# An expert weight ring of eight groups instead of six, with loops over four experts

## The chip, the cores and the metric

The program runs on one core of one Trainium2 chip. The metric is the device time of one execution in microseconds, from the runs of the whole program; the profile is of one such execution. PE is the TensorE (matrix) engine, DVE the VectorE, ACT the ScalarE, POOL the GpSimd engine, and SP the SyncE, which issues most of the DMA transfers. SBUF is the on-chip memory of 128 partitions, PSUM the accumulators of PE (8 banks of 512 fp32 values a partition).

## What is computed

Two blocks on x, 256 tokens of 1024 features, all in fp32. The first block has two attentions, a gated merge, then 32 routed experts and a small gate (PLE); the second block is two layers of convolution and pooling with a modulation made from c. The experts carry most of the weights: each has 1024 x 2048 for gate and up and 1024 x 1024 for down, 12 MB, 402 MB in all.

```python
def hybrid_layer(...):
    ...
    merged = sigmoid(gate_a) * (y_a @ w_branch_a) + sigmoid(gate_b) * (y_b @ w_branch_b)
    x = x + merged @ w_out
    x = x + routed_experts(rmsnorm(x, g_ffn), w_router, b_router, w_gate_up, b_gate_up, w_down, b_down)
    hp = rmsnorm(x, g_ple)
    x = x + sigmoid(hp @ w_ple_gate) * (p_i @ w_ple_proj)

# an expert, on the tokens that chose it (top 4 of 32)
gu = xb @ w_gate_up[e] + b_gate_up[e]
g, u = minimum(gu[:, :1024], 7.0), clip(gu[:, 1024:], -7.0, 7.0)
y = ((u + 1.0) * g * sigmoid(1.702 * g)) @ w_down[e] + b_down[e]

# second block, per layer l
mod = silu(c) @ w_ada[l] + b_ada[l]          # shift, scale, gate
h = rms_norm(x, g_pre[l]) * (1 + scale) + shift
```

## The kernel before

Each engine has its own hand-written program; they meet only through semaphores. SP issues the weight loads in one fixed order, in three phases, through one SBUF tile, ring, of 12 slots of 1 MB (P x 2048 fp32).

- Phase 1 (to about 270 us): the projections, both attentions, the merge, w_out, the router. 48 chunks of 1 MB go through the 12 slots (chunks1, the semaphore chunk_used1 counts those that PE is done with). Among them are 24 chunks of w_ada_2, whose products run between the others on PE (ada_parts) into PSUM bank 7. ACT copies these sums out (ada_out), SP moves them with 16 small DMAs within SBUF (ada_moved, lines 414 to 418), PE adds and transposes them (mod_sums) and DVE makes the columns of the modulation (mod_columns). For layer 0 that is done between the attentions, for layer 1 the moves are issued ahead of the experts and mod_sums and mod_columns run between PLE and the second block (PSUM use "ada1" of phase 3).
- Experts: 12 MB of an expert are six groups of 2 MB (GROUPS): q = 0 to 3 for gate/up, 4 and 5 for down. Group q always goes to slots 2q and 2q+1 of ring, with a semaphore ring2[q]. SP's function expert(e, used) waits for each group until PE has counted chunk_used2 up to the use of the same slots by the expert before, then issues the load. The first expert's groups wait for the phase-1 chunks in the same slots (phase1_left). Behind them SP issues ada_moved(1), then loops over the other 31 experts.
- PE's loop, like those of DVE and ACT, takes two experts a pass (PAIRS): for each, two bias products, the gate/up product over 8 slots of K (side_by_side, line 1551, 64 matmul instructions), the gather of the next pair's tokens (gather), transposes, the down product (32 instructions). Tokens that an expert gets are selected with a one-hot matrix (pick) and its result is scattered back onto X by another product. A loop over more rounds is for experts with over 64 tokens (extra).
- Ahead of the loop: DVE chooses the experts (choose, shares), counts positions, makes pick; PE gathers the first pair's tokens into PSUM pair 1; DVE copies them to xg (gathered, line 1038); PE waits for ada_out, bias_ready, routed, then enters the loop and waits for xg_ready.
- Phase 3: PLE and the two layers, 37 chunks of 1 MB through slots 0 to 7 (chunks3). The first eight wait for the last expert's groups in the same slots.

Besides ring there is the arena, 72 KB a partition, whose regions are reused from phase to phase; view(kb, n) is n fp32 values from kb on. In phase 1 gate A lies at 0 to 8, gate B at 24 to 32, q and k of the second attention from 36 to 48, merged at 48 to 56, scratch SQ from 56, SW from 62, probabilities from 66. In the experts xg, glu, sig, upc, hid, hidT lie from 0 to 14, scat and pickw from 18, esel, bias, then yslot at 40 to 44 and tok_high from 48. raw_bias, the expert biases as loaded, lies at 62. POOL loads raw_bias after y_done (both attentions ready), ACT casts it to bias (line 624), DVE makes its low part (line 1004), then clears yslot and scat, then adds w_out's product to X (x_sum, line 932).

Of the kernel before, what the change touches and what calls it, by code (L numbers as in the profile page):

```python
# [7 lines left out]
S, D = 256, 1024  # L8
HALVES = S // P
# [19 lines left out]
GROUPS = SLOTS // 2  # L29
# [59 lines left out]
def build(nc, t, out):  # L89
# [8 lines left out]
    with ctx:  # L98
# [58 lines left out]
        ada_rows = [view(24, 512), view(36, 512)]  # L157
        ada_mods = [view(26, 512, "p (r n) -> p r n", r=4), view(38, 512, "p (r n) -> p r n", r=4)]
# [21 lines left out]
        lg, mask, ex, em, pm = [SQ[:, 64 * i:64 * i + 64].rearrange("p (a b) -> p a b", a=HALVES) for i in range(5)]  # L180
        top_v = SQ[:, 320:336].rearrange("p (a b) -> p a b", a=HALVES)
        top_f = SQ[:, 336:352].rearrange("p (a b) -> p a b", a=HALVES)
# [25 lines left out]
        pin = view(57, HALVES * 256, "p (a b) -> p a b", a=HALVES)  # L208
        pT = view(59, 2 * S, "p (a b) -> p a b", a=2)
# [32 lines left out]
        ring2 = [sem(f"ring2_{i}") for i in range(GROUPS)]  # L242
# [28 lines left out]
        def used1(name):  # L271
# [9 lines left out]
                             ("o1", 2, used1("o1")), ("fT0", 0, N), ("fT1", 2, N)])  # L281
        ADA_BANK = 7
        U3, _, _ = ordinals([("pT", 2, N), ("pp0", 0, 1), ("pp1", 2, 1), ("hT0", 1, N), ("hT1", 3, N),
                             ("g0", 1, 3), ("g1", 3, 5), ("ada1", 0, N)])
# [109 lines left out]

        def slot1(n, a, b):
            return ring[:, n % SLOTS1, 0:a * b].rearrange("p (a b) -> p a b", a=a)
# [11 lines left out]
        def _(sp):  # L408
# [19 lines left out]
            def expert(e, used):  # L428
                for q in range(GROUPS):
                    used(q)  # L430
                    two = ring[:, 2 * q:2 * q + 2, :]
                    if q < 4:
                        src = gu_v[ds(e, 1), q].rearrange("e p k n -> (e p) k n")
                        sp.dma_start(two, src).then_inc(ring2[q], 16)
                    else:
                        src = dn_v[ds(e, 1), q - 4].rearrange("e p j n -> (e p) j n")
                        sp.dma_start(two.rearrange("p a (b n) -> p (a b) n", b=2), src).then_inc(ring2[q], 16)
# [5 lines left out]
            expert(0, phase1_left)  # L443
            ada_moved(1)
            with sp.Fori(0, E - 1) as before_e:
                expert(before_e + 1, lambda q: sp.wait_ge(s["chunk_used2"], before_e * GROUPS + (q + 1)))
            sp.wait_ge(s["routed"], 1)
            extra = sp.value_load(nextra[0:1, 0:1], min_val=0, max_val=ROUNDS - 1)
            with sp.If(extra > 0):
                with sp.Fori(0, extra) as r:  # L450
                    with sp.Fori(0, E) as e:
                        expert(e, lambda q: sp.wait_ge(s["chunk_used2"],
                                                       r * (E * GROUPS) + e * GROUPS + ((E - 1) * GROUPS + q + 1)))
# [13 lines left out]
        def _(pool):  # L467
# [40 lines left out]
            pool.wait_ge(s["y_done"], 2)  # L508
# [11 lines left out]
            pool.dma_start(pin, t["p"][0, 0].rearrange("(h p) n -> p h n", p=P)).then_inc(s["p_in"], 16)  # L520
            pool.dma_start(invw, t["inv_windows"]).then_inc(s["inv_in"], 16)
            for z, n in ((U, PAD), (Z, 2)):
                G.memset(z[:, :, 0:n], 0.0).then_inc(s["pads_set"], 1)
            power(0, 2)
            filled3(pool, "ada1")
            for z in (WA, WB):
# [1237 lines left out]
```

## Time and profile before

| | us |
|---|---|
| median of 3 runs | 1474.71 |
| lowest and highest | 1472.77, 1475.29 |
| the profiled execution | 1472.31 |
| its span, first to last instruction | 1470.2 |
| PE busy | 1358.9 (92%) |
| DVE, ACT, POOL busy | 424.4, 274.2, 29.3 |
| chain that ended last | PE 58%, DMA 28%, issue 8%, DVE 3% |

Mean granted clock of PE over the span: 0.977 of full speed. A time in the rows is in microseconds from the span's start, if not marked ns. PEld is PE's weight load, SPq the DMA issues of SP. "[1.51 <-DVE ...]" behind an instruction says that its engine sat idle for 1.51 us before it, and which instruction ended that. Of a busy PE the ends are modelled.

### The profile page before, as it was taken

Reading aid. Unit: us, or ns where it says so; the run is one execution under the profiler, and the core shown is the slowest. Engines: PE = TensorE matmul, PEld = TensorE weight load, DVE = VectorE, ACT = ScalarE, POOL = GpSimd, SP = SyncE. Lnnn points to the kernel's source line nnn. Section 1 sums busy time; section 2 is a strip of 40 time slices with the busy share of each in tenths; the row PEclk is TensorE's granted clock in tenths of the full one; section 3 lists DMA queues with packets and bytes.
Section 4 is the critical chain, followed back from the end, with each engine's and each line's share of the span. In section 5 each row is a group of like instructions: output and inputs, shape, how many; then the busy total and the mean of one; then the engine's idle time right before and its main releaser. Section 6 shows DMA issues by size and latency. Waiting matters only on the chain.

```text
span 1470.2 us, 16175 instructions
## 1 busy us (share of the span) xinstructions
PE 1358.9 (92%) x6558; PEld 676.5 (46%) x6558; DVE 424.4 (29%) x656; ACT 274.2 (19%) x387; POOL 29.3 (2%) x46
## 2 busy tenths in 40 slices
PE   4999999899999999999899999998999989898897
PEld 2446544443333333333333333333333336896896
DVE  0416223421122112112111121121111216675773
ACT  2032222211101101101010011010100114532531
POOL 1100010000000000000000000000000000000000
PEclk9999999899999999999999999999999999899999
DMA  8894266699999999999999999999999996355330
GB/s 313 310 344 150 86 209 241 270 407 428 428 428 429 428 429 428 429 429 428 428 428 428 429 428 428 428 428 429 429 428 430 428 412 224 105 181 199 111 119 29
DMA packets 76663, 498.64 MB, mean 339 GB/s; under 512 B 6919, under 2 KB 8282, under 8 KB 52058
## 3 DMA queue, kind: packets, MB, share of 16 engines
q1 hardware_dynamic: 73360, 494.43, 82.2%
q0 software_dynamic: 704, 2.10, 0.4%
q10 hardware_dynamic: 2570, 1.70, 0.4%
q8 instruction: 22, 0.36, 0.1%
q14 instruction: 7, 0.06, 0.0%
HBM read 497.06 MB, written 1.05 MB: 339 GB/s over the span
## 4 chain that ended last, share of the span: by engine, by line
PE 58%; DMA 28%; issue 8%; DVE 3%; ACT 1%; ACTq 0%; POOL 0%; DVEq 0%; SPq 0%; POOLq 0%
PE ps L1551 28%; DMA ring<-in_w_gate_up_dram 28%; PE ps L1323 7%; PE ps L1650 3%; PE ps L1652 3%; PE ps L1651 3%; PE ps L1545 2%; PE ps L1483 2%; PE ps L1467 2%; PE ps L1333 1%; PE ps L1302 1%; PE ps L1532 1%; PE ps L1614 1%; PE ps L1555 1%; ACT arena L651 1%
## 5 line engine op out<-in xcount | busy, mean ns | idle before, releaser
L1551 PE MATMUL ps<-ring,arena 128*64 128x512 f32 x3072 | 697.6, 605 | 38.8 <-DMA ring<-in_w_gate_up_dram 25.6
L1551 PEld LDWEIGHTS ps<-ring,arena 128*64 128x64 f32 x3072 | 213.1, 139 | 487.9 <-issue 400.3
L1082 DVE TENSOR_SCALAR arena<-ps 128x512 f32<-128x512 f32 x32 | 22.1, 692 | 350.2 <-PE ps L1551 350.2
L644 ACT ACTIVATE arena<-arena 128x512 f32<-128x512 f32 x32 | 20.2, 630 | 505.3 <-DVE arena L1082 505.3
L1323 PE MATMUL ps<-ring,HT 128*128 128x512 f32 (+1 forms) x256 | 111.7, 589 | 0.0
L1652 PE MATMUL ps<-arena_highs,w_low 128*128 128x256 f32 x384 | 108.4, 282 | 0.0
L1043 DVE TENSOR_SCALAR esel<-const 128x128 fp32r<-128x128 f32 x49 | 12.6, 285 | 283.3 <-ACT arena L655 145.9
L655 ACT COPY arena<-ps 64x512 f32<-64x512 f32 x64 | 37.2, 581 | 242.1 <-PE ps L1551 241.7
L1061 DVE TENSOR_TENSOR X<-X,ps 128x1024 f32<-128x1024 f32 x34 | 41.4, 1217 | 124.1 <-PE ps L1545 124.1
L1650 PE MATMUL ps<-arena_highs,ring_highs 128*128 128x256 f32 x256 | 72.7, 284 | 1.8 <-DVE HT_r L1120 1.8
L1323 PEld LDWEIGHTS ps<-ring,HT 128*128 128x128 f32 x256 | 48.2, 191 | 54.5 <-issue 54.1
L1652 PEld LDWEIGHTS ps<-arena_highs,w_low 128*128 128x128 f32 x384 | 73.1, 190 | 0.0
L1651 PE MATMUL ps<-HT_r,ring_highs 128*128 128x256 f32 x256 | 72.3, 282 | 0.0
L1545 PE MATMUL ps<-arena 128*128 128x512 f32 x136 | 67.5, 618 | 2.6 <-DVE X L1061 1.3
L1532 PE MATMUL ps<-pick,tok_high 128*128 128x128 f32 x272 | 65.4, 288 | 1.7 <-issue 1.7
L1532 PE MATMUL ps<-pick,tok_low 128*128 128x128 f32 x272 | 64.1, 283 | 0.0
L1532 PEld LDWEIGHTS ps<-pick,tok_high 128*128 128x128 f32 x272 | 53.5, 200 | 14.7 <-issue 14.7
L1103 DVE TENSOR_TENSOR w_low<-ring,ring_highs 128x2048 fp32r<-128x2048 f32 x26 | 58.3, 2286 | 1.0 <-POOL st L498 0.8
L1532 PEld LDWEIGHTS ps<-pick,tok_low 128*128 128x128 f32 x272 | 53.6, 200 | 0.0
L664 ACT CAST ring_highs<-ring 128x2048 fp32r<-128x2048 f32 x26 | 48.2, 1907 | 22.2 <-PE ps L1652 22.2
L1650 PEld LDWEIGHTS ps<-arena_highs,ring_highs 128*128 128x128 f32 x256 | 49.1, 192 | 2.0 <-issue 2.0
L1651 PEld LDWEIGHTS ps<-HT_r,ring_highs 128*128 128x128 f32 x256 | 48.8, 191 | 0.0
(233 smaller groups left out, 1222.7 us busy)
## 6 DMA issues: line engine op xcount, KB each, us to landing
ring<-in_w_gate_up_dram SPq DMA_DIRECT2D x128, 2048.0 KB, 24.2
ring<-in_w_down_dram SPq DMA_DIRECT2D x64, 2048.0 KB, 21.4
ring<-in_w_in_dram SPq DMA_DIRECT2D x38, 1024.0 KB, 7.0
ring<-in_w_ada_dram SPq DMA_DIRECT2D x24, 1024.0 KB, 9.2
ring<-in_w_out_dram SPq DMA_DIRECT2D x12, 1024.0 KB, 6.1
ring<-in_w_ple_gate_dram SPq DMA_DIRECT2D x4, 1024.0 KB, 23.4
ring<-in_w_branch_a_dram SPq DMA_DIRECT2D x2, 1024.0 KB, 9.7
ring<-in_w_branch_b_dram SPq DMA_DIRECT2D x2, 1024.0 KB, 9.8
```

The lines of the kernel that those rows point to most:

```text
L655: last = A.copy(yslot[g][at:at + CAP, :], ps[at:at + CAP, 5, :])
L664: A.copy(high_of(m), slot3(n)).then_inc(s["w_highs"], 1)
L1061: V.tensor_tensor(X[:, h, :], X[:, h, :], flat(3), ALU.add).then_inc(s["sc_used"], 1)
L1103: V.tensor_tensor(slot3(m + 1, w_low), slot3(m + 1), high_of(m).bitcast(fp32), ALU.subtract).then_inc(s["w_lows"], 1)
L1323: last = T.matmul(ps[:, 2 * p + h, 0:n], HT[:, 4 * kh + k, h * P:h * P + P], slot1(c, 4, n)[:, k, :], start=kh + k == 0, stop=4 * kh + k = ...
L1467: last = T.matmul(ps[:, 2 * p + h, :], HT[:, 4 * br + k, h * P:h * P + P], slot1(c, 4, 512)[:, k, :], start=k == 0, stop=k == 3)
L1532: return T.matmul(ps[:, 2 + j, k % 4 * P:k % 4 * P + P], part[:, h, k, :], pick[:, h].rearrange("p e n -> p (e n)"), start=first, stop=h = ...
L1545: last = T.matmul(ps[:, 6 + g, :], scat[:, h, g, :], yslot[g], start=True, stop=True)
L1551: last = T.matmul(ps[at:at + CAP, bank, :], lhsT, w(g), start=False, stop=stop)
L1650: T.matmul(out, lhs[0], rhs[0], start=first, stop=False, skip_group_check=True)
L1651: T.matmul(out, lhs[0], rhs[1], start=False, stop=False, skip_group_check=True)
L1652: return T.matmul(out, lhs[1], rhs[0], start=False, stop=last, skip_group_check=True)
```

## The change

- The groups go round through eight places of 2 MB (BINS) instead of six: load number s of an expert quartet goes to place s mod 8. Places 0 to 5 are the ring, places 6 and 7 (more_bins) are regions of the arena, 32 to 48 and 56 to 72. ring2 has eight semaphores, and PE waits for 16 times the number of loads of that place.
- SP issues the first loads of places 6 and 7 (groups 0 and 1 of expert 1) behind a wait for y_done, ahead of those of places 0 to 5; ada_moved(1) stands behind the sixth load as before. Its loops go over four experts (QUADS, PER_QUAD = 24 groups).
- PE's loop goes over four experts, two pairs one after the other; DVE's and ACT's loops stay at two.
- To free the arena: ada_rows[1] and ada_mods[1] move to 20 and 16, the router's scratch to 24.5, tmp of the merge to 16, yslot to 4 and the experts' other scratch to 8, raw_bias to 0, pin and pT into tabs. As raw_bias now lies over gate A, POOL loads it after merged_done.
- mod_sums and mod_columns of layer 1 leave phase 3 and stand ahead of the expert loop: on PE behind the first gather (in place of the wait for ada_out), on DVE behind gathered(). They use PSUM pair 2 ("mod1").
- POOL clears the pads and loads inv_windows behind w_highs, that is behind the experts.
- The first eight chunks of phase 3 wait for the last uses of places 0 to 3.

```diff
-GROUPS = SLOTS // 2
+GROUPS = 6
+BINS = 8
+QUADS = E // 4
+PER_QUAD = 4 * GROUPS
...
+        scratch = arena[:, 24 * 256 + 128:26 * 256]
...
-        glu, sig, upc, hid, hidT = [view(4 + 2 * i, 512) for i in range(5)]
-        yslot = [view(40 + 2 * i, 512) for i in range(2)]
+        yslot = [view(4 + 2 * i, 512) for i in range(2)]
+        glu, sig, upc, hid, hidT = [view(8 + 2 * i, 512) for i in range(5)]
...
-        raw_bias = view(62, 3 * 512)
+        raw_bias = view(0, 3 * 512)
+        more_bins = [view(32, 2 * SLOT, "p (a b) -> p a b", a=2), view(56, 2 * SLOT, "p (a b) -> p a b", a=2)]
...
+        def bin2(s):
+            b = s % BINS
+            return ring[:, 2 * b:2 * b + 2, :] if b < SLOTS // 2 else more_bins[b - SLOTS // 2]
...
-            def expert(e, used):
-                for q in range(GROUPS):
-                    used(q)
-                    two = ring[:, 2 * q:2 * q + 2, :]
...
+            def load(e, s):
+                q, two = s % GROUPS, bin2(s)
...
+            def quad(e, used):
+                for s in range(PER_QUAD):
+                    used(s)
+                    load(e + s // GROUPS, s)
...
-            expert(0, phase1_left)
-            ada_moved(1)
-            with sp.Fori(0, E - 1) as before_e:
-                expert(before_e + 1, lambda q: sp.wait_ge(s["chunk_used2"], before_e * GROUPS + (q + 1)))
+            sp.wait_ge(s["y_done"], 2)
+            for k in range(GROUPS, BINS):
+                load(1, k)
+            for k in range(PER_QUAD):
+                if k < GROUPS:
+                    phase1_left(k)
+                elif k >= BINS:
+                    sp.wait_ge(s["chunk_used2"], k - BINS + 1)
+                if k < GROUPS or k >= BINS:
+                    load(k // GROUPS, k)
+                if k == GROUPS:
+                    ada_moved(1)
+            with sp.Fori(0, QUADS - 1) as i:
+                quad(i * 4 + 4, lambda k: sp.wait_ge(s["chunk_used2"], i * PER_QUAD + (PER_QUAD + k - BINS + 1)))
...
-                    sp.wait_ge(s["chunk_used2"], extra * (E * GROUPS) + ((E - 1) * GROUPS + n // 2 + 1))
+                    sp.wait_ge(s["chunk_used2"], extra * (E * GROUPS) + (E * GROUPS - BINS + n // 2 + 1))
...
-            pool.wait_ge(s["y_done"], 2)
+            pool.wait_ge(s["merged_done"], 2)
...
+            pool.wait_ge(s["w_highs"], 1)
+            for z, n in ((U, PAD), (Z, 2), (WA, PAD), (WB, PAD)):
+                G.memset(z[:, :, 0:n], 0.0).then_inc(s["pads_set"], 1)
             pool.dma_start(invw, t["inv_windows"]).then_inc(s["inv_in"], 16)
...
             gathered()
+            mod_columns(1, filled(dve, "mod1"), moved1, U1["mod1"][2] + 1)
...
-            mod_columns(1, filled3(dve, "ada1"), moved3, 1)
...
-            pe.wait_ge(s["ada_out"], 8)
+            mod_sums(1, free(pe, "mod1"), full1)
...
-            with pe.Fori(0, extra * PAIRS + PAIRS) as i:
+            def pair_of_experts(i, s0, loaded):
...
-                            pe.wait_ge(ring2[k // 2], n * 16 + 16)
+                            two = loaded(s0 + e * GROUPS + k // 2)
...
+            with pe.Fori(0, extra * QUADS + QUADS) as i:
+                def loaded(k):
+                    pe.wait_ge(ring2[k % BINS], i * (16 * PER_QUAD // BINS) + 16 * (k // BINS + 1))
+                    return bin2(k)
+
+                pair_of_experts(i * 2, 0, loaded)
+                pair_of_experts(i * 2 + 1, 2 * GROUPS, loaded)
...
-            mod_sums(1, U3["ada1"][0], full3)
```

## Rows read from the trace of the kernel before

**Rows 1.** The page: share of the DMA engines in 40 slices, in tenths.
```profile
DMA  8894266699999999999999999999999996355330
```

**Rows 2.** Windows, the long stretch: busy us of each engine, granted clock, DMA share, GB/s.
```profile
320.00:1180.00 860.00, 809.04 (x3714) 309.48 (x3712) 158.43 (x255) 99.18 (x150) 0.00 (x0) 0.98 1.01 429
```

**Rows 3.** Chain that ended last: start us, us, what; the experts.
```profile
329.97 7.96 PE ps L1551 x32
...
497.51 7.09 PE ps L1551 x32
...
521.39 24.79 DMA ring<-in_w_gate_up_dram
...
931.87 25.49 DMA ring<-in_w_gate_up_dram
...
961.23 25.50 DMA ring<-in_w_gate_up_dram
...
1200.31 7.11 PE ps L1551 x32
```

**Rows 4.** Timeline of SP, its DMA issues: start us, us from first to last, line, operation.
```profile
224.05 0.37 SPq L426 DMA_DIRECT2D ring<-in_w_ada_dram  x1
...
269.87 11.64 SPq L418 DMA_DIRECT2D arena<-arena  x16
286.16 12.68 SPq L434 DMA_DIRECT2D ring<-in_w_gate_up_dram  x4
307.48 3.77 SPq L437 DMA_DIRECT2D ring<-in_w_down_dram  x2
```

**Rows 5.** Windows ahead of the loop and in it, columns as in rows 2.
```profile
240.00:252.00 12.00, 12.00 (x35) 5.77 (x34) 1.88 (x4) 1.66 (x4) 0.57 (x1) 1.00 0.10 22
...
282.00:283.00 1.00, 1.00 (x4) 0.24 (x2) 0.00 (x0) 0.00 (x0) 0.00 (x0) 0.50 0.02 3
283.00:284.00 1.00, 1.00 (x4) 0.24 (x2) 0.00 (x0) 0.00 (x0) 0.00 (x0) 0.50 0.00 0
...
284.00:288.00 4.00, 4.00 (x22) 1.32 (x20) 0.00 (x0) 0.00 (x0) 0.00 (x0) 1.00 0.30 66
```

**Rows 6.** Timeline of PE, its first instructions of the expert loop.
```profile
279.56 1.19 PE L1555 MATMUL ps<-bias,esel 128*128 128x512 f32 x2 [1.51 <-DVE arena L1038]
```

**Rows 7.** Timeline of PE, the modulation's sums of layer 0.
```profile
147.41 1.07 PE L1345 MATMUL ps<-const,arena 24*128 24x24 f32 x8
```

**Rows 8.** The biases and their neighbours: timelines of DVE, ACT, PE; DMA landings.
```profile
225.38 1.22 DVE L922 TENSOR_TENSOR arena<-arena 128x1024 f32<-128x1024 f32 x1
...
230.44 1.49 ACT L624 CAST bias<-arena 128x1536 fp32r<-128x1536 f32 x1
...
232.03 3.53 DVE L1004 TENSOR_TENSOR bias<-arena,bias 32x1536 fp32r<-32x1536 f32 x2 [5.42 <-ACT bias L624]
...
236.82 0.48 DVE L1009 MEMSET arena<- 128x512 f32 x1
243.75 1.29 DVE L932 TENSOR_TENSOR X<-X,ps 128x512 f32<-128x512 f32 x2 [6.44 <-PE ps L1483]
...
250.41 1.04 PE L1494 MATMUL ps<-const,X 128*128 128x128 f32 x8
...
L515 POOL DMA_DIRECT2D arena<-in_b_down_dram x4: 511/511/525, 192.7 to 195.8; - x4
...
arena<-in_p_dram POOLq DMA_DIRECT2D x1, 256.0 KB, 5.8
wr<-in_w_router_dram ACTq DMA_DIRECT2D x1, 128.0 KB, 14.4
```

**Rows 9.** Timeline of PE between PLE and the first layer.
```profile
1253.89 3.36 PE L1302 MATMUL ps<-const,HN 128*128 128x128 f32 x16 [6.53 <-DVE HN L1187]
```

**Rows 10.** The chain at the first back edge; the page's queue of instructions.
```profile
337.94 0.66 PE ps L1555 x2
...
q8 instruction: 22, 0.36, 0.1%
```

More of the change, by code:

```diff
@@ L156, in build @@
         hn_flat = HN[:].rearrange("p a b -> p (a b)")
-        ada_rows = [view(24, 512), view(36, 512)]
-        ada_mods = [view(26, 512, "p (r n) -> p r n", r=4), view(38, 512, "p (r n) -> p r n", r=4)]
+        ada_rows = [view(24, 512), view(20, 512)]
+        ada_mods = [view(26, 512, "p (r n) -> p r n", r=4), view(16, 512, "p (r n) -> p r n", r=4)]
         gate = [view(0, HALVES * D, "p (a b) -> p a b", a=HALVES), view(24, HALVES * D, "p (a b) -> p a b", a=HALVES)]
@@ L241, in build @@
         ring1 = [sem(f"ring1_{i}") for i in range(SLOTS1)]
-        ring2 = [sem(f"ring2_{i}") for i in range(GROUPS)]
+        ring2 = [sem(f"ring2_{i}") for i in range(BINS)]
         ring3 = [sem(f"ring3_{i}") for i in range(SLOTS3)]
@@ L426, in _ @@
                 sp.dma_start(slot1(n, a, b), src).then_inc(ring1[n % SLOTS1], 16)
-            def expert(e, used):
-                for q in range(GROUPS):
-                    used(q)
-                    two = ring[:, 2 * q:2 * q + 2, :]
[L432 to L437, printed above, removed]
+            def load(e, s):
+                q, two = s % GROUPS, bin2(s)
+                if q < 4:
+                    src = gu_v[ds(e, 1), q].rearrange("e p k n -> (e p) k n")
+                    sp.dma_start(two, src).then_inc(ring2[s % BINS], 16)
+                else:
+                    src = dn_v[ds(e, 1), q - 4].rearrange("e p j n -> (e p) j n")
+                    sp.dma_start(two.rearrange("p a (b n) -> p (a b) n", b=2), src).then_inc(ring2[s % BINS], 16)
+            def quad(e, used):
+                for s in range(PER_QUAD):
+                    used(s)
+                    load(e + s // GROUPS, s)
             def phase1_left(q):
@@ L450, in _ @@
                 with sp.Fori(0, extra) as r:
-                    with sp.Fori(0, E) as e:
-                        expert(e, lambda q: sp.wait_ge(s["chunk_used2"],
-                                                       r * (E * GROUPS) + e * GROUPS + ((E - 1) * GROUPS + q + 1)))
+                    with sp.Fori(0, QUADS) as i:
+                        quad(i * 4, lambda k: sp.wait_ge(s["chunk_used2"], r * (E * GROUPS) + i * PER_QUAD
+                                                         + (E * GROUPS + k - BINS + 1)))
             for n, (src, a, b) in enumerate(chunks3):
                 if n < SLOTS3:
-                    sp.wait_ge(s["chunk_used2"], extra * (E * GROUPS) + ((E - 1) * GROUPS + n // 2 + 1))
+                    sp.wait_ge(s["chunk_used2"], extra * (E * GROUPS) + (E * GROUPS - BINS + n // 2 + 1))
                 else:
@@ L1005, in _ @@
                                 ).then_inc(s["bias_ready"], 1)
+            dve.wait_ge(s["bias_ready"], 2)
             run(V.memset(posm[:, :, PCOLS:PCOLS + 2], -1.0))
@@ L1583, in _ @@
                         if k % 2 == 0:
-                            pe.wait_ge(ring2[k // 2], n * 16 + 16)
+                            two = loaded(s0 + e * GROUPS + k // 2)
                         x = xg[:, k, e * CAP:e * CAP + CAP]
-                        side_by_side(0, x, lambda g: ring[:, k, g * 512:g * 512 + 512], 0, k == KC - 1)
-                        last = side_by_side(1, x, lambda g: ring[:, k, F + g * 512:F + g * 512 + 512], 0, k == KC - 1)
+                        side_by_side(0, x, lambda g: two[:, k % 2, g * 512:g * 512 + 512], 0, k == KC - 1)
+                        last = side_by_side(1, x, lambda g: two[:, k % 2, F + g * 512:F + g * 512 + 512], 0, k == KC - 1)
                         if k % 2:
@@ L1619, in _ @@
                     for f in range(2):
-                        pe.wait_ge(ring2[4 + f], n * 16 + 16)
-                        w = ring[:, 8 + 2 * f:10 + 2 * f, :].rearrange("p a (b n) -> p (a b) n", b=2)
+                        w = loaded(s0 + e * GROUPS + 4 + f).rearrange("p a (b n) -> p (a b) n", b=2)
                         for j in range(4):
```

21 lines of the change are left out of this document (8 added, 13 removed).

## The prediction

> **What bounds the kernel now.** I read the page's 40 slices first. The DMA line stands at 9 (90% or more) from the ninth slice to the thirty-third and lower before and after [rows 1]: there is one long stretch in which the weights of the experts arrive without a break, and room ahead of it. The window from 320 to 1180 us puts a number on it: 429 GB/s at a DMA share of 1.01 [rows 2]. One group of expert weights is 2,097,152 bytes, so it takes 4.89 us at that rate.
>
> The chain of waits says who ends last. From 521.39 us on it is a ladder of two rungs: a gate/up group is on its way for 25.5 us, then PE multiplies 16 instructions with it, then SP issues the load that takes its place [rows 2, 3]. Two issues of the ladder are 961.23 - 931.87 = 29.36 us apart. That is six groups, the depth of the ring, so 4.89 us a group again. Before 521 the chain runs through PE alone: the down product of the first pair of experts starts at 329.97 and that of the fourth at 497.51, three pairs in 167.54 us, 55.85 us a pair [rows 3]. The DMA needs 12 x 4.894 = 58.7 us for the same pair. PE thus eats up the lead that the full ring gave it, 2.9 us a pair, and from then on waits for every group. The end of the experts is set by the DMA queue, not by PE.
>
> When did that queue last stand still? Not at the start of the program but around the first pair. All six groups have landed by 280 us; the queue then moves 3 GB/s or less until PE has used the first one and SP can issue the seventh load, at 286.16. The loads that follow are issued at 286.16 (the first of four), ..., 307.48 (the eleventh load, freed by the fifth group) [rows 4, 5]. A model of one line holds all of it: load k+6 can't start before use k, and every later load costs 4.894 us. The end is the largest use(k) - 4.894 k, plus 186 x 4.894. For k = 0 that gives 286.16, for k = 4 it gives 307.48 - 19.58 = 287.90, the larger. So the end of the stream is 287.90 + 910.3 = 1198.2. PE's last down product starts at 1200.31, after its hidden activations, and ends at 1207.4 [rows 3]. The model closes.
>
> **The two groups more.** They are issued by SP after the last chunk of the first phase, whose issue is at 224.05 [rows 4], not during the second attention: SP works in order, and its wait for y_done has long been met. The four chunks still under way and the two groups then fill the queue, and groups 0 and 1 behind them arrive up to 9.8 us later, by about 248. From 240 to 252 the queue moved 22 GB/s [rows 5], so the room is there, and the first use is at 280. Groups 2 to 5 wait for chunks of the first phase as before. In the formula 186 loads after the first use become 184: **-2 x 4.894 = -9.8 us**, if PE starts as before.
>
> **PE does not start as before.** The sums of the second layer's modulation (mod_sums) move from the end of the PLE stage to just ahead of the expert loop, and PE waits there for all sixteen small moves of ada_rows to ada_mods. In the kernel before nobody waited for these until 1246. SP issues them from 269.87, one every 0.70 to 0.73 us, for 11.64 us, that is until 281.51 [rows 4]. The queue is empty of weights by then, and its last traffic falls between 282 and 283, none between 283 and 284 [rows 5]. PE began the loop at 279.56, after 1.51 us of idleness, released by the DVE's gather copy, so its gather ended at 278.05 [rows 6]. Now it stands until about 282.5 (bounds 282.0 and 283.1). The eight sum instructions took 1.07 us for the first layer at full clock [rows 7]; here the granted clock is 0.50, that is 1.2 GHz, until 284 [rows 5], so 1.07 to 2.14, and I take 1.5. The loop starts at 284.0 instead of 279.56: **+4.4 us** (+3.5 to +5.7). Queued behind the wait on PE is the whole loop. On the DVE, mod_columns stands behind the gather copy and waits for PE's sums; the selections behind it are wanted only at the first pair's second expert.
>
> The clock belongs to that stretch. Before, it was at 0.50 for the first 4.4 us of the loop, until 284, then at 1.00 [rows 5, 6]. With a wait of 4 us more ahead of the loop it will be low at the start again. Between no low stretch in the loop and one of 8 us the cost against before is -2.2 to +1.8 us; I take 0, as the same work follows. All of this passes on in full, since use(4) moves by as much as PE's start.
>
> Sum: -9.8 + 4.4 = **-5.4 us** (bounds: -9.8 + 3.5 - 2.2 = -8.5 and -9.8 + 5.7 + 1.8 = -2.3). One expert pair after another PE will then lead for (9.8 / 2.9) three pairs more, and the ladder of the chain begins near 700 instead of 521.
>
> **The biases** are loaded after merged_done instead of after y_done, since they now lie where gate A lay. POOL's eight issues follow each other at 0.52 us (every second one is of b_down, from 192.7 to 195.8); the DVE's sum that releases them ends at 226.6, so the last is issued 3.6 us later, at 230.2. They now run beside full weight traffic. The nearest row for that is the load of p, 5.8 us from issue to landing: they land at 236.0. ACT's cast of 1.49 us waits for them, the DVE's 3.53 us and its three memsets of 0.48 us follow: done at about 242.5. The DVE's residual sum of half 0, queued behind them, starts at 243.75 when PE has its product [rows 8]. **Cost 0**, under a cover of 1.2 us there, and another 5 us until PE wants the sum's columns at 250.4. With the 14.4 us of the router's load at the start of the program, the farthest row, they would land at 244.6 and that sum start at 251.1, 7.4 us late.
>
> **The PLE stage.** Removed are mod_sums on PE and mod_columns on the DVE between PLE and the first layer. PE waits 6.53 us there for the normalised rows whichever way [rows 9], and the DVE's three small instructions lie beside ACT's sums of squares: 0. POOL's memsets and its load of inv_windows (512 KB, 1.2 us of the queue) move behind the experts; the table is first read after the first layer's product. The chunks of the last phase are issued two groups earlier relative to the last use, and move with the stream: 0. Removing a wait for a lead that nothing needs can't gain.
>
> **The loop over four experts.** It halves the back edges. The first back edge of the kernel before costs nothing: the down product that starts at 329.97 ends at 337.93 and the next pair's bias product starts at 337.94 [rows 3, 10]. So nothing can be gained. It may cost: the pass grows from about 250 matmuls and as many weight loads to twice that. Bounds for a back edge are 0 and the 5.8 us of a loaded landing; I take 0, the row of the same branch. On SP the unrolled waits cost nothing, since five groups are always queued ahead.
>
> What the Trainium skill has on this ("Runtime: NRT & Kernel Launch", Instruction fetch mechanics): PE's instruction memory is 128 KiB, 2,048 instructions, filled in blocks of 256; a note below it says that only two blocks are held and that a taken branch out of them stalls for a fetch. By the first the four experts fit and the sum stands; by the second it would grow by the stall of the rival below. The trace's back edge of some 500 instructions without a gap doesn't contradict either.
>
> **The rivals.**
> - Refetch: PE doesn't hold the longer pass, and each of the seven back edges stalls. For it: the instruction queue carried only 22 packets, 0.36 MB, so nothing of the trace shows a pass of this length held; against it: the free back edge now [rows 10]. A PE that never waited for weights would end at 284.0 + 16 x 55.85 = 1177.6, the stream lets it end at 1207.4 - 5.4 = 1202.0; the stalls hide in 24.4 us, 3.5 us each. At 5.8 us each, 40.6 - 24.4 = 16.2 us show: 1474.7 - 5.4 + 16.2 = 1485.5. It ends slower than before from 4.3 us a stall. Chance 0.12.
> - The start loses all: the moves, the biases or the clock cost 9.8 instead of 4.4 (the biases at 14.4 us, with 2 of their 7.4 us hidden by PE's product, would do it). Then 1474.7, range 1472 to 1478. For it: the cover of 1.2 us; against it: 5 us of cover behind that. Chance 0.18.
> - The start loses nothing, because the moves are in when PE asks: 1474.7 - 9.8 = 1464.9. Against it speak SP's last issue at 281.5 and traffic until 282 [rows 4, 5]. Chance 0.07.
> - The two groups don't come early enough or the queue isn't the bound (the change doesn't do what it says): 1474.7 + 4.4 = 1479.1. Against it: rows 2 and 5. Chance 0.03.
>
> **How the numbers follow.** The profiled execution took 1472.3 us with a span of 1470.2; the median of the runs is 1474.7, 2.4 more. The difference of 5.4 is taken off both: 1466.9 for the profiled one, **1469.3** for the median, chance 0.60, its own range 1466.2 to 1472.4. About 0.2%, 2.9 us, is what a measurement of this kernel can tell. The forecast's range reaches into that at its upper end. Faster: 0.54 of the forecast and 0.07 of the third rival, and a little of the second, 0.63. Slower: 0.12 x 0.8 of the first, 0.03 of the last and 0.03 of the second, 0.15. Within: 0.22. The range for 8 in 10 leaves out most of the refetch and of the lossless start: 1465.0 to 1478.0.
>
> **What the profile of the changed kernel would show.** Two issues of gate/up groups near 224.5; SP's sixteen moves from 270; PE idle from 278 to 282.5, then L1345's eight instructions, then the loop near 284; the ninth load near 290.6; queue still between 280 and 290; the ladder of waits with rungs of 8 groups, 39.2 us less the multiplication, that is landings of about 35 us after their issue; the last down product ending near 1202; no gap over 1 us at PE's back edges. Wrong would be: PE's start not moved, or moved by over 6 us; a granted clock low for over 8 us of the loop; gaps at every fourth expert; a rate in the stream other than 429 GB/s.

## The result

The changed kernel takes 1477.84 us (median of 10 runs, 1477.12 to 1481.72) against 1474.21 us before (10 runs, 1471.89 to 1475.84): ratio 1.003, 95% interval 1.002 to 1.004. It is **slower by 3.6 us**, where 5.4 us less was forecast: the other way than forecast, though still just inside the stated range of 1465.0 to 1478.0. The profiled execution took 1477.57 us with a span of 1475.3 us, 5.1 more than before.

SP's issues in the profile after (timeline: start us, us from first to last, line, operation), to be held against [rows 4]:

```profile
223.46 0.37 SPq L435 DMA_DIRECT2D ring<-in_w_ada_dram  x1
223.87 0.98 SPq L441 DMA_DIRECT2D arena<-in_w_gate_up_dram  x2
225.32 44.64 SPq L441 DMA_DIRECT2D ring<-in_w_gate_up_dram  x4
...
279.37 11.25 SPq L427 DMA_DIRECT2D arena<-arena  x16
301.05 3.77 SPq L441 DMA_DIRECT2D ring<-in_w_gate_up_dram  x2
309.98 3.76 SPq L444 DMA_DIRECT2D ring<-in_w_down_dram  x2
322.39 3.76 SPq L441 DMA_DIRECT2D ring<-in_w_gate_up_dram  x2
```

The two additional groups are issued at 223.87, as forecast. But everything behind is late: the sixteen moves start at 279.37 instead of 269.87, the first load that a use sets free at 301.05 instead of 286.16, the one freed by the fifth use at 322.39 instead of 307.48. PE's timeline shows the start of the loop [rows 6, 7]:

```profile
257.36 1.97 PE L1515 MATMUL ps<-const,X 128*128 128x128 f32 x8 [7.38 <-DVE X L952]
...
291.81 1.87 PE L1366 MATMUL ps<-const,arena 24*128 24x24 f32 x8 [4.26 <-DMA arena<-arena]
293.61 1.22 PE L1576 MATMUL ps<-bias,esel 128*128 128x512 f32 x2
```

PE stands idle twice: 7.38 us for the DVE's residual sum of half 0, which before was ready in time, and 4.26 us for the moves. The loop starts at 293.61 instead of 279.56. Behind each wait the granted clock is at its lower level of 1.2 GHz for a while (windows, columns as in rows 2); in the loop that lasts until 300, 6.4 us instead of 4.4:

```profile
260.00:264.00 4.00, 4.00 (x8) 1.75 (x7) 2.13 (x2) 3.29 (x2) 0.00 (x0) 0.69 0.00 0
...
296.00:300.00 4.00, 4.00 (x12) 1.00 (x10) 0.89 (x3) 0.00 (x0) 0.00 (x0) 0.50 0.00 0
300.00:304.00 4.00, 4.00 (x22) 1.24 (x18) 0.00 (x0) 0.00 (x0) 0.00 (x0) 1.00 0.53 172
```

The chain that ended last names what the DVE waited for (start us, us, what):

```profile
226.32 0.73 POOL arena L535
...
230.16 18.95 DMA arena<-in_b_down_dram
249.13 1.48 ACT bias L644
250.71 1.75 DVE bias L1024
252.49 1.77 DVE bias L1024
256.02 1.30 DVE X L952 x2
```

The last bias load takes 18.95 us to land, where in the kernel before the median of its kind took 2.7. The cast, the low part, the memsets and the residual sum follow, the latter at 256.02 instead of 243.75 [rows 8].

The stream of weights runs at the same rate as before [rows 2], as the window from 320 to 1180 us shows (columns as in rows 2):

```profile
320.00:1180.00 860.00, 811.93 (x3760) 312.48 (x3758) 158.40 (x255) 99.39 (x150) 0.00 (x0) 0.99 1.01 428
```

The last down product of the experts starts 4.86 us later than before, at 1205.17 [rows 3]. The chain that ended last, in the experts:

```profile
722.08 34.59 DMA ring<-in_w_gate_up_dram
...
1205.17 7.11 PE ps L1572 x32
```

The ladder of waits begins at 722 instead of 521, with landings of about 35 us: the deeper ring does what it should, after a start that is 14 us late.

### The profile page after: what moved, and what is told of

Same layout as the page of the kernel before. It is cut to its first block, busy times and chain, and to the rows that moved or that the text cites. A ratio compares the mean times of both kernels' runs of the same rounds, so it can differ in the third digit from the quotient of the medians.

```text
span 1475.3 us, 16032 instructions
## 1 busy us (share of the span) xinstructions
PE 1356.9 (92%) x6558; PEld 678.9 (46%) x6558; DVE 424.4 (29%) x656; ACT 274.4 (19%) x387; POOL 29.2 (2%) x46
## 4 chain that ended last, share of the span: by engine, by line
PE 62%; DMA 23%; issue 8%; DVE 3%; ACT 2%; SPq 1%; POOL 1%; ACTq 0%; DVEq 0%; POOLq 0%
PE ps L1572 32%; DMA ring<-in_w_gate_up_dram 18%; PE ps L1344 7%; PE ps L1566 3%; PE ps L1677 3%; PE ps L1679 3%; PE ps L1678 3%; DMA arena<-in_w_gate_up_dram 2%; PE ps L1488 2%; PE ps L1553 1%; DMA arena<-in_b_down_dram 1%; PE ps L1354 1%; PE ps L1635 1%; PE ps L1323 1%; PE ps L1576 1%
## 5 line engine op out<-in xcount | busy, mean ns | idle before, releaser
L1572 PE MATMUL ps<-ring,arena 128*64 128x512 f32 x2304 | 518.8, 601 | 30.2 <-DMA ring<-in_w_gate_up_dram 19.1
L1572 PEld LDWEIGHTS ps<-ring,arena 128*64 128x64 f32 x2304 | 160.0, 138 | 361.7 <-issue 305.1
L1572 PE MATMUL ps<-arena 128*64 128x512 f32 x768 | 175.0, 608 | 5.2 <-ACT arena L671 3.3
L1572 PEld LDWEIGHTS ps<-arena 128*64 128x64 f32 x768 | 53.7, 139 | 117.1 <-issue 102.5
```

Of the source, the lines that this page charges most:

```text
L1572: last = T.matmul(ps[at:at + CAP, bank, :], lhsT, w(g), start=False, stop=stop)
```

## The experiments

The theory after the result: one gain and two costs add up, and they meet in one number, the time of the fifth use. (1) The ring's two groups take 2 x 4.894 us from the stream. (2) The late biases hold the residual sum and all that follows. (3) The moves and the sums hold the loop. Rivals: the clock, or one of the two costs being covered by the other; the deeper ring giving nothing. Four kernels undo (2), (3), both, or move the two groups; of the next four, bias_half leaves out half of the bias loads and three put one part of the change alone into the kernel before; two change who issues what. All medians stand beside runs of the kernel before on the same chip: 1474.02 for the first four, 1474.86 for the next four, 1474.34 for the last two.

### bias_early: the biases loaded early again

```diff
-        raw_bias = view(0, 3 * 512)
+        raw_bias = view(18, 3 * 512)
-            pool.wait_ge(s["merged_done"], 2)
+            pool.wait_ge(s["y_done"], 2)
-            tmp = view(16, HALVES * 512).rearrange("p (a b) -> p a b", a=HALVES)
+            tmp = view(12, HALVES * 512).rearrange("p (a b) -> p a b", a=HALVES)
```

> The changed kernel with one thing undone: raw_bias lies at 18 to 24 of the arena and tmp of the merge at 12, so that POOL loads the biases after y_done as in the kernel before, ahead of the weight groups. Theory (the biases, 19.0 us from issue to landing behind 8 MB of weights, hold DVE's residual sum of half 0 and the whole start): they land before 200, PE's transposes of half 0 follow the products without the 7.38 us of idleness, the gather ends near 277.5, the sixteen moves land near 281.6, the loop starts near 283.6 instead of 293.68, and as use(4) sets the stream the median falls by the same 10 us, from 1477.8 to 1467.8. Rival (the moves or the clock alone set the start, the biases are covered): loop start after 290, 1474 to 1478.

Measured: **1468.84 us** (1467.97 to 1470.37), ratio 0.9961 (0.9947 to 0.9974). PE's timeline:

```profile
250.22 1.04 PE L1515 MATMUL ps<-const,X 128*128 128x128 f32 x8
...
282.13 1.87 PE L1366 MATMUL ps<-const,arena 24*128 24x24 f32 x8 [4.26 <-DMA arena<-arena]
283.93 1.22 PE L1576 MATMUL ps<-bias,esel 128*128 128x512 f32 x2
```

The first wait is gone, the second stands unchanged. The biases' move cost 9.0 us of the median, and the change without it is faster than the kernel before.

### sums_late: the modulation's sums after PLE again

```diff
-        ada_rows = [view(24, 512), view(20, 512)]
+        ada_rows = [view(24, 512), HT[:, 0:2, :].rearrange("p a b -> p (a b)")]
-        ada_mods = [view(26, 512, "p (r n) -> p r n", r=4), view(16, 512, "p (r n) -> p r n", r=4)]
+        ada_mods = [view(26, 512, "p (r n) -> p r n", r=4), const[:, C_CAUSAL:C_CAUSAL + 512].rearrange("p (r n) -> p r n", r=4)]
...
+            act.wait_ge(s["ada_in"], 512)
...
-            mod_columns(1, filled(dve, "mod1"), moved1, U1["mod1"][2] + 1)
...
+            mod_columns(1, filled3(dve, "ada1"), moved3, 1)
...
-            mod_sums(1, free(pe, "mod1"), full1)
+            pe.wait_ge(s["ada_out"], 8)
...
+            mod_sums(1, U3["ada1"][0], full3)
```

> The changed kernel with the other thing undone: the sums and columns of the second layer's modulation stand between PLE and the second block again (ada_rows in HT, the moved rows in const, both free there), the biases stay late. Theory: the biases still cost what they cost, the wait of 4.26 us and the sums of 1.87 us ahead of the loop go, less the 1.4 us that the gather copy takes anyway: loop start near 289.0 instead of 293.68, median 1473.2. Rival (the wait for the moves only fills time that the late biases would cost anyway through the clock): 1476 to 1478.

Measured: **1473.13 us** (1471.34 to 1475.65), ratio 0.9995 (0.9985 to 1.0004), as expected. The loop starts at 288.73; the biases still hold PE by 6.69 us.

### both

Both edits together.

> Both undone: early biases and the modulation sums between PLE and the second block; the eight groups and the loop over four experts stay. Theory: PE starts the loop near 279.0 as in the kernel before, and the two groups more shorten the stream by 2 x 4.894 = 9.8 us: median 1474.2 - 9.8 = 1464.4, last down product starting near 1190 to 1191. Rival (the deeper ring gives nothing by itself, or the longer loop costs): 1470 to 1475.

Measured: **1464.49 us** (1463.05 to 1465.18), ratio 0.9926 (0.9912 to 0.994): 9.5 us faster than the kernel before. PE's timeline at the start of the loop:

```profile
279.38 1.19 PE L1577 MATMUL ps<-bias,esel 128*128 128x512 f32 x2 [1.51 <-DVE arena L1060]
```

The chain that ended last, at the last down product:

```profile
1189.89 7.11 PE ps L1573 x32
```

The loop starts as in [rows 6], the product 10.4 us earlier than in [rows 3]. This is what the ring of eight is worth when PE starts on time, and it is the fastest kernel of the study. The four medians (after, bias_early, sums_late, both) also show that the two costs add, within the spread of the runs: undoing the biases brings 9.0 us beside early sums and 8.6 beside late ones; undoing the sums 4.7 and 4.4.

### groups_last: the two groups behind the moves

```diff
-            sp.wait_ge(s["y_done"], 2)
-            for k in range(GROUPS, BINS):
-                load(1, k)
...
                 if k == GROUPS:
                     ada_moved(1)
+                    sp.wait_ge(s["y_done"], 2)
+                    for j in range(GROUPS, BINS):
+                        load(1, j)
```

> The changed kernel with the two additional groups issued behind the sixteen small moves instead of ahead of group 0; late biases and early sums stay. Theory (the biases drip in beside queued weights and end when these end): only the last chunks and groups 0 and 1 are queued beside them, until about 240; the biases land near 240, DVE is ready near 247, covered by PE until 250; the loop starts near 283.6, the two groups land in the dead time 282 to 293: median 1467.8, as bias_early. Rival (a load by POOL after merged_done is slow whatever is queued): biases land after 245, 1474 to 1478. Rival (groups 6 and 7 must be early): 1475 or more.

Measured: **1474.27 us** (1472.13 to 1477.64), ratio 0.9999 (0.9989 to 1.0009). It is a miss: 1467.8 was expected, and the median lies in the range of the first rival, a load that is slow behind merged_done whatever is queued. The cast of the biases starts at 244.79 instead of 249.13, so fewer queued groups do help, but it is 5 us later than I had put it, and PE still waits for 3.18 us. The fifth use comes at 318.72, 3.7 us before that of the changed kernel, and the median falls by 3.6. (The profiled execution, 1476.71 us, is one of the slower ones of this kernel.) That the two additional groups come 63 us later does no harm: from the fifth use to the last down product it takes 882.9 us here and 882.8 in the changed kernel. PE's timeline:

```profile
253.02 1.97 PE L1515 MATMUL ps<-const,X 128*128 128x128 f32 x8 [3.18 <-DVE X L952]
...
288.20 1.87 PE L1366 MATMUL ps<-const,arena 24*128 24x24 f32 x8 [4.67 <-DMA arena<-arena]
```

### bias_half: half the packets

```diff
-                for r0 in (64 * g, 64 * g + E):
+                for r0 in (64 * g,):
...
-            act.wait_ge(s["bias_in"], 16 * 8)
+            act.wait_ge(s["bias_in"], 16 * 4)
```

> The changed kernel with four of the eight bias loads (only the rows of which the high part is made; the rows for the low part hold old values, so the result is off by that). Theory (each packet of the biases waits its turn beside 16 KB packets of weights, so the landing goes with the number of packets): 96 data packets instead of 192 drip in over about 9 instead of 17.6 us, landing near 239, DVE ready near 245, loop start near 284, median 1468. Rival (the biases wait until the weights queued before them are through, whatever their number): last landing stays near 249, 1477.8.

Measured: **1468.78 us** (1467.98 to 1469.38), ratio 0.996 (0.9945 to 0.9975). It leaves out the rows from which the low parts are formed, four of the eight loads. The landings of the four b_gate_up and the four b_down loads in the changed kernel (one line's instructions, us from issue to landing):

```profile
DMA to landing us min/median/max: 7.8/12.7/17.4
...
DMA to landing us min/median/max: 8.5/14.4/19.0
```

The same of the two and two loads of bias_half:

```profile
DMA to landing us min/median/max: 7.7/9.4/11.1
...
DMA to landing us min/median/max: 8.4/10.3/12.2
```

It comes out as the theory had it. The loads don't wait for one moment and then land together. The eight issued from 226.3 to 230.2 land from 234.1 (226.3 + 7.8) to 249.1, one every 2.1 us ((249.1 - 234.1) / 7); the four issued from 227.2 to 229.0 land from 234.9 to 241.2, one every 2.1 us too (averages). It is a drip whose length goes with what is to be carried, not a gate that opens when the weights queued before are through. The edit halves loads, packets and bytes together, so this run alone doesn't say which of them counts. The windows of bias_half, columns as in rows 2, show the rate come back when the last of them is in:

```profile
236.00:240.00 4.00, 4.00 (x11) 1.73 (x10) 0.00 (x0) 0.00 (x0) 0.00 (x0) 1.00 1.03 338
240.00:244.00 4.00, 4.00 (x11) 1.85 (x10) 1.19 (x1) 1.47 (x1) 0.00 (x0) 1.00 0.99 422
```

### bias_late: the biases late in the kernel before

```diff
-            pool.wait_ge(s["y_done"], 2)
+            pool.wait_ge(s["merged_done"], 2)
```

> The kernel before with one thing changed: POOL loads the biases after merged_done instead of after y_done. The queue holds only the last chunks and groups 0 and 1 then, until about 238 to 240. Theory (drip beside queued weights): last landing near 240, 9 to 10 us after its issue, DVE ready near 247, behind 243.75 but ahead of PE's transposes at 250.4: 0 to 1 us, median 1474.2 to 1475.2. Rival (19 us whatever is queued): landing near 250, +7 to +9 us, 1482.

Measured: **1480.24 us** (1478.94 to 1480.89), ratio 1.0036 (1.0023 to 1.0049): 5.4 us slower, where at most 1 was expected: neither the theory nor its rival (7 to 9) had it. Without the two additional groups in the queue the last landing takes 14.2 us, not 9 to 10. The windows of this kernel show why the queue did not run dry by 240 (columns as in rows 2):

```profile
232.00:236.00 4.00, 4.00 (x11) 1.76 (x10) 0.00 (x0) 0.00 (x0) 0.00 (x0) 1.00 0.98 327
236.00:240.00 4.00, 4.00 (x10) 1.71 (x9) 0.00 (x0) 0.00 (x0) 0.00 (x0) 1.00 1.00 322
240.00:244.00 4.00, 4.00 (x11) 1.83 (x10) 0.00 (x0) 0.00 (x0) 0.00 (x0) 1.00 0.84 226
```

While the biases drip, the DMA engines are as busy as ever (share about 1.0) and carry a quarter less than the 429 GB/s of [rows 2]. So the small loads also hold up the weights beside which they wait. The residual sum starts at 252.15 instead of 243.75; the cover of 250.4 [rows 8] is missed by 2.58 us of PE's idleness, and PE's clock falls to 0.50 behind it (timeline, then a window with columns as in rows 2):

```profile
253.49 1.61 PE L1494 MATMUL ps<-const,X 128*128 128x128 f32 x8 [2.58 <-DVE X L932]
...
254.00:256.00 2.00, 2.00 (x8) 1.48 (x7) 0.56 (x2) 1.48 (x4) 0.57 (x1) 0.50 0.96 410
```

PE's loop starts at 284.38, 4.8 us late. The transposes are 3.1 us late (253.49 instead of 250.41), and the way from them to the end of the gather takes 29.4 us instead of 27.6, which is the clock's part.

### sums_first: the sums first in the kernel before

```diff
-            pe.wait_ge(s["ada_out"], 8)
+            mod_sums(1, free(pe, "mod1"), full1)
...
+            mod_columns(1, filled(dve, "mod1"), moved1, U1["mod1"][2] + 1)
```

> The kernel before with one thing changed: mod_sums and mod_columns of the second layer stand ahead of the expert loop as in the changed kernel. Theory: the moves are in at 282.3, the sums take 1.87 us at the low clock, loop start 284.1 instead of 279.56, the stream and the median move by the same: 1474.2 + 4.6 = 1478.8 (with the clock's share 1477 to 1480.5). Rival (PE's start has slack against the stream): 1474.2.

Measured: **1480.83 us** (1479.13 to 1482.08), ratio 1.004 (1.0026 to 1.0054): 6.0 us slower. The loop starts at 284.70, 5.1 us late, and the first freed load is issued at 292.22 instead of 286.16, 6.1 us late: the granted clock stays at 0.50 until 291, for 6.3 us of the loop instead of 4.4. The 5.1 us lie within the prediction's bounds for this term, towards the upper end, and the clock's share in the loop, which it put at 0, is 0.9. With that the median is 0.3 us above the range expected for this run.

### loop_four: PE's loop alone

```diff
-            with pe.Fori(0, extra * PAIRS + PAIRS) as i:
+            def pair_of_experts(i):
...
+            with pe.Fori(0, extra * (PAIRS // 2) + PAIRS // 2) as j:
+                pair_of_experts(j * 2)
+                pair_of_experts(j * 2 + 1)
```

> The kernel before with PE's loop over four experts and nothing else. Theory (PE holds the longer pass; back edges free; the stream is the bound): median 1474.2 within 1 us, no gap at the back edge between the fourth expert's down product and the next bias product, 23 to 25 packets of instructions. Rival (refetch): a gap of 1 to 6 us at every second pair in the first five pairs, over 40 packets of instructions.

Measured: **1474.32 us** (1473.19 to 1476.28), ratio 1.0001 (0.9991 to 1.001): no difference. The page's queue of instructions:

```profile
q8 instruction: 24, 0.39, 0.1%
```

24 packets against 22 in [rows 10], for eight passes; the rival asked for over 40. Its chain has no gap at the first back edge, from the fourth expert's down product to the next bias product:

```profile
385.98 7.09 PE ps L1551 x32
393.07 0.66 PE ps L1555 x2
```

The same count stands on the page of the changed kernel, whose chain shows its first back edge, from the down product to the bias product of the fifth expert, without a gap:

```profile
401.25 7.09 PE ps L1572 x32
408.34 0.67 PE ps L1576 x2
```

### moves_shared: half the moves issued by ACT

The edit is on top of bias_early:

```diff
-                for r in range(4):
+                for r in range(4) if l == 0 else range(2):
...
             ada_out(1)
+            act.wait_ge(s["ada_out"], 8)
+            for r in range(2, 4):
+                for c in range(4):
+                    act.dma_start(ada_mods[1][ADA_COLS * c:ADA_COLS * c + ADA_COLS, r, :],
+                                  ada_rows[1][32 * r:32 * r + ADA_COLS, c * P:c * P + P]).then_inc(s["ada_in"], 16)
```

> bias_early (median 1468.84, loop start 283.93) with one thing changed: eight of the sixteen small moves are issued by ACT behind its copies, eight by SP. Theory (SP's issue rate of 0.70 us a move sets when PE may sum): the last move is issued near 275.5 and 276 and PE's wait after the gather shrinks from 4.26 us to 0 to 2 us, the latter if the moves on SP's queue come in only behind group 5, which lands near 279.5; loop start 279.8 to 281.7, median 1464.5 to 1466.6. Rival (the moves are late because of what is queued in the DMA engines, not of their issue): wait stays over 4 us, 1468.8.

Measured: **1466.35 us** (1465.74 to 1467.03), ratio 0.9948 (0.9931 to 0.9965), 2.5 less than bias_early, which ran on another chip. The traces show less: the loop starts 1.4 us earlier than in bias_early (282.56 instead of 283.93) and the fifth use comes 0.6 earlier, so the rest of the 2.5 is not explained by the moves. The issues end 5.0 us earlier (275.88 on ACT instead of 280.92), the wait shrinks by 1.5. SP's share of the moves in its timeline:

```profile
269.83 5.67 SPq L427 DMA_DIRECT2D arena<-arena  x8
```

PE's first sum of the modulation:

```profile
280.76 1.87 PE L1371 MATMUL ps<-const,arena 24*128 24x24 f32 x8 [2.74 <-DMA arena<-arena]
```

So the rate of issue set 1.5 us of the wait, and close behind it lies a second limit: the moves are in only 4.8 us after the last issue. The weight traffic queued ahead of them ends near 278; whether that is the limit was not tried. My range of 0 to 2 us for the remaining wait was short by 0.7, that for the loop's start by 0.9.

### bias_on_act: the biases on ACT's queue

```diff
-            pool.wait_ge(s["merged_done"], 2)
...
-                    pool.dma_start(rows[:, 1024:1536], t["b_down"][0, :, g * 512:g * 512 + 512]
-                                   ).then_inc(s["bias_in"], 16)
...
+            act.wait_ge(s["merged_done"], 2)
...
+                    act.dma_start(rows[:, 1024:1536], t["b_down"][0, :, g * 512:g * 512 + 512]
+                                   ).then_inc(s["bias_in"], 16)
             act.wait_ge(s["bias_in"], 16 * 8)
```

> The changed kernel with one thing changed: ACT, on its hardware queue, issues the eight bias loads after merged_done, behind its copies of the merged columns (about 230 to 235), in place of POOL. Theory (packets of a second queue drip in beside the weights' 16 KB packets, whichever engine issued them): last landing after 246, 12 us or more after its issue, PE idle before the transposes of half 0 by 5 to 10 us, median 1476 to 1481. Rival (POOL's software queue is what is slow): landing within 5 us of the issue, by 240, PE not idle, median 1468 to 1470.

Measured: **1483.12 us** (1482.94 to 1483.92), ratio 1.0065 (1.0048 to 1.0082), 2 us above the expected range. On ACT's hardware queue the loads are no faster: issued from 228.75 to 233.19, the last one landed 21.1 us after its issue (19.0 on POOL's queue), cast at 254.30. PE's wait is 12.71 us, where 5 to 10 were expected:

```profile
262.53 1.97 PE L1515 MATMUL ps<-const,X 128*128 128x128 f32 x8 [12.71 <-DVE X L952]
```

The rival, that POOL's queue is what is slow, is out. ACT's queue is no cure, it is somewhat worse: it issues later and lands later.

## Why the prediction was wrong

**Right: the model of the stream.** The end of the experts is the fifth use plus the loads that follow. Over nine of the twelve kernels (the other three lie at 882.9, 883.0 and 883.0; chain: start of the last down product; timeline of SP: issue after the fifth use):

| kernel | groups | fifth use, us | last down product, us | difference |
|---|---|---|---|---|
| before | 6 | 307.48 | 1200.31 | 892.8 |
| bias_late | 6 | 311.92 | 1204.77 | 892.9 |
| sums_first | 6 | 313.55 | 1206.70 | 893.2 |
| loop_four | 6 | 307.61 | 1200.70 | 893.1 |
| after | 8 | 322.39 | 1205.17 | 882.8 |
| bias_early | 8 | 311.08 | 1193.90 | 882.8 |
| sums_late | 8 | 316.54 | 1199.34 | 882.8 |
| both | 8 | 307.01 | 1189.89 | 882.9 |
| groups_last | 8 | 318.72 | 1201.57 | 882.9 |

The difference is 892.8 to 893.2 with six groups and 882.8 to 882.9 with eight, about 10.1 us less; the term was -9.8. It says the ring was worth what was forecast, and that every microsecond of a late fifth use passes on in full to the end of the experts.

**Right, somewhat short: the wait for the moves.** Forecast +4.4 (+3.5 to +5.7) and the clock -2.2 to +1.8. In the changed kernel PE's gather ends at 287.55 (291.81 less 4.26), the loop starts 6.06 us later instead of 1.51: +4.5. The sums took 1.87 us, not 1.5, at the low clock. Undone, it gives back 4.7 and 4.4 us; alone in the kernel before it costs 6.0: 5.1 at the loop's start and 0.9 in the loop, where the clock stays low longer.

**Right: the loop over four** (0; loop_four), and, as far as can be seen, **the PLE stage** (0). From the last down product to the end of the span the twelve profiles take 269.9 to 273.2 us, with the sums in the one place and in the other alike; this scatter of 3.3 us would hide a small cost. The rival of a refetch, 0.12, had no part in it. The Trainium skill's two statements on it ("Runtime: NRT & Kernel Launch", Instruction fetch mechanics) differ; loop_four's 24 packets and its gapless back edge agree with the larger memory.

**Wrong: the cost of the late biases.** The step is the sentence that took 5.8 us, the landing of p, as the nearest row, and 14.4 us as the farthest. It measured 18.95, outside both ends, and the 0 became 9 us (9.0 and 8.6 by the four medians). p was the wrong neighbour: the weights' traffic ends near 279, so p, issued at 273.5, was helped by a queue that ended 6 us later. The biases are issued at 226 to 230 into a queue which the same prediction, in its part on the two groups, had filled until 248. The two statements were never put side by side. Had they been, the bound would have been that the small loads may drip until the queue is empty, 248, and with the 6.9 us from landing to residual sum in the chain of after (256.02 - 249.11) that sum would have come out at 254.9; it came at 256.02. That would have been close partly by luck: the queue ends at 248 in bias_early (share 0.30 from 248 to 252), but in the changed kernel it is still full then (0.97, last window below), because the biases hold the weights up too. The cover of 1.2 us, and 5 us behind it, was named rightly; what was to be covered was not.

The landing, taken with the rest of its chain: 249.1 instead of 236.0 is 13.1 us; about 1.2 are hidden by the wait for half 0's product, 5 by PE's further product, which leaves 6.9: 7.38 us of idleness measured. Then PE's clock falls to half, and the work from the transposes to the end of the gather takes 30.19 us instead of 27.64. This is a second gap of the step: the prediction priced the clock in the loop only, and ahead of it the clock cost 2.5 us. The start was 14.05 us late in all; counted from the last chunk of phase 1, which was issued 0.6 us earlier than before, 14.6 us, of which 4.5 are the moves' and 10.1 the biases' (7.5 until the transposes, 2.5 by the clock).

The sum with the measured terms: -10.05 for the ring, +4.55 for the moves, +10.09 for the biases, -0.59 for the earlier phase 1, +0.86 for the clock in the loop (from the loop's start to the fifth use 28.78 us instead of 27.92) gives +4.86, by which the expert stage ends later. The median moved by 3.6 and the profiled executions by 5.3; the difference lies within the scatter of the stage behind the experts.

The second rival (start costs 9.8 instead of 4.4, named with the biases at 14.4 us; chance 0.18, range 1472 to 1478) is the mechanism that came true, at a larger price. Its own sum was wrong: of the 7.4 us, 5.4 would have been hidden by PE's product and 2 would have shown, not the other way round; with bias_late's fall of the clock (1.7 us behind a wait of 2.58) that is some 4 us. That 1477.84 lies in its range is therefore partly luck.

Of the signs of being wrong that the prediction lists, one came: PE's start moved by over 6 us. The clock was low for 6.4 us of the loop, not over 8, the loop over four had no gap, and the stream's rate was 428 GB/s.

**The drip.** The theory that stood up is of small packets that take turns with large ones: landings spread evenly (bias_half), on either issuing engine (bias_on_act), ending with their own number. In bias_late, where the queue has less in it, the last lands sooner, at 245.3 (231.1 + 14.2), soon after the windows show the traffic run out. The changed kernel's DMA queues can be counted (packets, MB, share of 16 engines' time): q1 carries the weights, q0 the biases. From 226 to 250, from 232 to 248, and from 250 to 256, when the biases are in:

```profile
q0 software_dynamic: 320, 0.79, 9.7%
...
q1 hardware_dynamic: 306, 4.49, 88.5%
q0 software_dynamic: 289, 0.66, 12.5%
...
q1 hardware_dynamic: 172, 2.56, 100.2%
```

While the biases drip, the weights' queue moves 306 packets and theirs 289, about one for one. A turn of an engine is then 16 x 16 / 306 = 0.84 us, a load has 320 / 8 = 40 packets or 2.5 turns of each of the 16 engines, and 2.5 x 0.84 = 2.1 us, as measured. On ACT's queue the same 0.79 MB are 512 packets, and the last load lands later, so that packets seem to count rather than bytes. The Trainium skill ("DMA: Bandwidth & Descriptors", Queues, rings and completion order) says that each DMA engine goes round between the queues it has work for, packet by packet. The runs agree with turns. Why the total rate falls by a quarter stays open: the small packets take 12.5% of the engines' time, but a megabyte of weights also takes a third more of it than afterwards (16 x 0.885 / 4.49 = 3.15 us of all 16 engines instead of 6 x 1.002 / 2.56 = 2.35).

## What to carry to other kernels

Where the stream of loads is the bound, a deeper ring is worth its additional groups times their transfer time, less what it delays the first uses: work out which use the stream hangs on (here the fifth), and hold every edit that frees the memory against that one time. A small load that an engine waits for is better issued before large transfers are queued; another queue didn't help here. Beside full queues these eight loads landed one every 2.1 us from 7.8 us behind the first issue on, as long as the weights lasted; the landing of one load elsewhere in the trace is no price for the last of eight. When a step is moved, look for its wait in the trace of the place it moves to, not of the place it comes from.

## What the hardware showed that was not expected

- Eight loads of 64 and 128 KB beside queued loads of 2 MB: 19.0 us from the last one's issue to its landing; ahead of those loads 2.7, the median landing of the b_down loads in the kernel before. The DMA engines' share stays near 1.0 while the rate is 310 to 336 GB/s, where the long stretch has 428, and it comes back once they are in, at 249.1. Windows of the changed kernel, columns as in rows 2:

```profile
232.00:236.00 4.00, 4.00 (x10) 1.71 (x9) 0.00 (x0) 0.00 (x0) 0.00 (x0) 1.00 1.01 310
236.00:240.00 4.00, 4.00 (x11) 1.75 (x10) 0.00 (x0) 0.00 (x0) 0.00 (x0) 1.00 1.04 335
240.00:244.00 4.00, 4.00 (x11) 1.85 (x10) 0.00 (x0) 0.00 (x0) 0.00 (x0) 1.00 1.02 311
244.00:248.00 4.00, 4.00 (x10) 1.72 (x10) 0.00 (x0) 0.00 (x0) 0.00 (x0) 1.00 0.99 336
248.00:252.00 4.00, 1.99 (x5) 0.57 (x3) 1.29 (x1) 1.47 (x1) 0.00 (x0) 1.00 0.97 414
```

- Moving the same loads from POOL's software queue to ACT's hardware queue did not speed them up (median landings of the b_gate_up and b_down loads 15.2 and 17.4 us instead of 12.7 and 14.4).
- A move of 3 KB within SBUF takes an issuing engine 0.70 us; sixteen of them 11.3 us, more than two groups of 2 MB take to arrive.
- Behind an idle stretch of PE of 2.58 us (bias_late) the granted clock went from 1.00 to 0.50, that is from 2.4 to 1.2 GHz, and the work up to the end of the gather took 1.7 us more; behind 7.38 us (the changed kernel) it took 2.5 more.
